# Expert results added onto two sums per token in HBM by accumulating transfers, in place of eight slot rows that are fetched and weighted at the end

## The reference, cut to what matters

```python
T, D, TOP_K, N_EXPERTS, EXPERT_HIDDEN, EXPERT_BLOCK = 512, 1024, 8, 64, 256, 128

def routed_experts(t, top_i, top_w, w_gu, w_dn):
    """Exact token-choice dispatch: sort assignments by expert, pad each expert segment to EXPERT_BLOCK rows."""
    ...
    def one_block(args):
        rb, e = args
        return swiglu_2(t_pad[rb], w_gu[e], w_dn[e]).astype(jnp.float32)

    ys = lax.map(one_block, (rows.reshape(n_blk, EXPERT_BLOCK), blk_expert)).reshape(P, D)
    out = jnp.zeros((T + 1, D), jnp.float32).at[rows].add(ys * wts[:, None])
    return out[:T]

# moe_ffn: routed + shared;  second_block:
x = x + g2 * moe_ffn(h, ...)
return rmsnorm_2(x, final_g)
```

## Time and profile before

| | |
|---|---|
| median of 3 runs | 3413.61 us (3406.23 to 3413.91) |
| the profiled execution | 3413.78 us |
| its span, first to last instruction | 3411.9 us |
| mean granted TensorE clock | 0.983 |
| TensorE busy | 3300.3 us (97%) |
| software queue (GpSimd's transfers) | 20736 packets, 33.60 MB |
| HBM written | 41.94 MB |

### The profile page before, as it was taken

The page is one execution under the profiler, slowest core; times in us unless marked ns, Lnnn a source line. Parts: engine busy times, 40 slices in busy tenths (PEclk is TensorE's granted clock), DMA queues, the critical chain, the costliest instruction groups (busy, mean ns, idle before and its releaser), DMA issues.

```text
span 3411.9 us, 48654 instructions
## 1 busy us (share of the span) xinstructions
PE 3300.3 (97%) x16474; PEld 2667.5 (78%) x16474; DVE 1978.3 (58%) x2520; ACT 1757.1 (52%) x2126; POOL 1335.7 (39%) x670
## 2 busy tenths in 40 slices
PE   8999999999999999999999999999999999999996
PEld 6888887778888788888678888787866788888784
DVE  4335674653354433541563333457766799999898
ACT  5552335455523555321645533414562688888884
POOL 3444441144444344444144444343202344444441
PEclk9999999999999999999999999899999999999998
DMA  3224331022253222533322233222102899999997
GB/s 124 98 95 167 113 102 50 20 92 94 97 169 121 86 98 93 165 119 117 125 80 97 93 97 100 74 93 90 32 7 73 320 381 382 389 387 389 374 366 295
DMA packets 128100, 534.42 MB, mean 157 GB/s; under 512 B 24464, under 2 KB 24720, under 8 KB 100112
## 3 DMA queue, kind: packets, MB, share of 16 engines
q1 hardware_dynamic: 107136, 499.63, 41.2%
q0 software_dynamic: 20736, 33.60, 2.6%
q10 hardware_dynamic: 144, 0.08, 0.0%
HBM read 531.64 MB, written 41.94 MB: 168 GB/s over the span
## 4 chain that ended last, share of the span: by engine, by line
PE 60%; issue 24%; POOL 7%; DVE 5%; ACT 1%; DMA 1%; POOLq 0%; DVEq 0%; SPq 0%; ACTq 0%
PE ps L822 16%; PE ps L824 16%; PE ps L823 16%; POOL w_lo L1893 7%; PE ps L1304 2%; PE ps L984 1%; PE ps L1109 1%; PE ps L842 1%; PE ps L1009 1%; PE ps L994 1%; PE ps L1127 1%; PE ps L1055 1%; PE ps L1088 1%; PE ps L1288 0%; DMA big<-in_exp_gu 0%
## 5 line engine op out<-in xcount | busy, mean ns | idle before, releaser
L1893 POOL TENSOR_TENSOR w_lo<-stage_buf,w_hi 128x1024 fp32r<-128x1024 f32 (+1 forms) x396 | 969.5, 2448 | 1511.6 <-ACT w_hi L1461 1511.6
L1461 ACT ACTIVATE w_hi<-stage_buf 128x1024 fp32r<-128x1024 f32 (+1 forms) x396 | 413.9, 1046 | 1189.6 <-PE ps L824 1133.6
L822 PE MATMUL ps<-x_hi,w_hi 128*128 128x512 f32 x1984 | 776.9, 392 | 6.8 <-POOL w_lo L1893 5.6
L823 PE MATMUL ps<-x_lo,w_hi 128*128 128x512 f32 x1984 | 775.4, 391 | 0.0
L824 PE MATMUL ps<-x_hi,w_lo 128*128 128x512 f32 x1984 | 775.0, 391 | 0.0
L822 PE MATMUL ps<-hid,w_hi 128*128 128x512 f32 x1312 | 518.8, 395 | 3.0 <-issue 1.7
L824 PE MATMUL ps<-hid,w_lo 128*128 128x512 f32 x1312 | 511.6, 390 | 0.0
L823 PE MATMUL ps<-hid,w_hi 128*128 128x512 f32 x1312 | 510.8, 389 | 0.0
L822 PEld LDWEIGHTS ps<-x_hi,w_hi 128*128 128x128 f32 x1984 | 374.6, 189 | 88.4 <-POOL w_lo L1893 6.7
L824 PEld LDWEIGHTS ps<-x_hi,w_lo 128*128 128x128 f32 x1984 | 374.6, 189 | 78.6
L823 PEld LDWEIGHTS ps<-x_lo,w_hi 128*128 128x128 f32 x1984 | 374.5, 189 | 77.4
(11 more groups left out here) (403 smaller groups left out, 4994.4 us busy)
## 6 DMA issues: line engine op xcount, KB each, us to landing
stage_buf<-in_gu SPq DMA_DIRECT2D x176, 512.0 KB, 3.2
big<-in_exp_gu SPq DMA_DIRECT2D x72, 1024.0 KB
h_buf<-in_exp_gu SPq DMA_DIRECT2D x72, 1024.0 KB
s_buf<-in_exp_dn SPq DMA_DIRECT2D x72, 1024.0 KB
stage_buf<-in_down SPq DMA_DIRECT2D x64, 512.0 KB, 3.6
stage_buf<-in_down SPq DMA_DIRECT2D x32, 384.0 KB, 3.2
sil_buf<-in_ada SPq DMA_DIRECT2D x24, 512.0 KB, 4.2
tmp_buf<-in_ada SPq DMA_DIRECT2D x24, 512.0 KB, 4.2
```

The source lines that it names most:

```text
L822: nc.tensor.matmul(o, a_hi, b_hi, start=start, stop=False)
L823: nc.tensor.matmul(o, a_hi, b_lo, start=False, stop=False)
L1461: nc.scalar.activation(w_hi[s][:, 0:n], stage[s][:, 0:n], ACT.Copy).then_inc(upper_done, 1)
L1893: nc.gpsimd.tensor_tensor(w_lo[s][:, 0:n], stage[s][:, 0:n], w_hi[s][:, 0:n].bitcast(F32), ALU.subtract).then_inc(parted, 1)
```

## The change

Two tensors of 512 x 1024 in HBM, `token_sums0` and `token_sums1`, take the place of `slot_rows`. GpSimd writes zeros to them from `xg[1]`, and writes the weights from `slot_w` to a third tensor, `pair_weights`. For each block a new indirect gather fetches the weight of each row into a column `w_col[s]`; ScalarE multiplies by it while it copies the result out of PSUM; and GpSimd's transfer adds the rows onto the token's row of the sum of that s (`compute_op=ALU.add`), where the scatter wrote rows of their own. A block holds a token at most once. The table gets a third column for the token number of the add.

At the end SP loads the two sums, TensorE adds them in PSUM with the plain identity (16 matmuls of 512 columns where there were 24), and VectorE has two instructions a tile in place of four; g2 and x are applied to the shared expert's output ahead of that. The early row additions and the scaled identities go.

The diff, without the declarations of semaphores and the removed lines that the words above cover:

```diff
@@ block_kernel: buffers
-        rows = ([big[:, 12288 + r * D:12288 + (r + 1) * D] for r in range(4)] +
-                [h_buf[:, r * D:(r + 1) * D] for r in range(4)] + [big[:, r * D:(r + 1) * D] for r in range(4, 12)])
+        sums = [[b[:, t * D:(t + 1) * D] for t in range(TT)] for b in (big[:, 12288:16384], h_buf)]
...
+        OUT_AT, W_AT = 5, 3
+        table = mask[:, 1024:1024 + 3 * (BLOCKS + OUT_AT)].rearrange("p (b c) -> p b c", c=3)
+        tab_f, tab_o = table[:, 0:BLOCKS, 0], table[:, OUT_AT:OUT_AT + BLOCKS, 1]
+        tab_v = table[:, W_AT:W_AT + BLOCKS, 2]
+        w_col = [mask[:, 1406 + s:1407 + s] for s in range(2)]
@@ sync
-                    def fetch(row, t, k, done):
-                        sp.dma_start(row.bitcast(I32), dr["slots"][t, :, k, :]).then_inc(done, 16)
...
                     for s in range(2):
+                        for j in range(2):
+                            after(raw_parted[j], more * 2 + (3 + s))
+                    for s in range(2):
+                        after(o_out[s], more * 16 + 32)
                         for t in range(TT):
+                            sp.dma_start(sums[s][t], dr[f"sum{s}"][t * P:(t + 1) * P, :]).then_inc(sum_in[s][t], 16)
@@ tensor: sum_rows
+                for s in range(2):
+                    for t in range(TT):
+                        pe.wait_ge(sum_in[s][t], 16)
                         for c in range(2):
+                            last = nc.tensor.matmul(ps[:, 2 * t + c, :], eye[:, :], sums[s][t][:, c * T:(c + 1) * T],
+                                                    start=(s == 0), stop=(s == 1))
+                        if s == 1:
+                            last.then_inc(fin["mm"], 1)
@@ scalar: evacuate
-                        nc.scalar.activation(o_sb[s], ps_t[:, b * T:b * T + D], ACT.Copy).then_inc(bk["oev"], 1)
+                        act.wait_ge(w_in[s], i * 16 + 16)
+                        nc.scalar.activation(o_sb[s], ps_t[:, b * T:b * T + D], ACT.Copy, scale=w_col[s]).then_inc(bk["oev"], 1)
...
-                    act.wait_ge(bk["tx"], more_n * 2 + 4)
-                    for j, w in enumerate(eye_w):
-                        n = j // 3 * TOP_K + EARLY + j % 3
-                        last = nc.scalar.activation(w, eye[:, :], ACT.Copy, scale=slot_w[:, n:n + 1])
@@ gpsimd
                     for s in range(2):
                         link(nc.gpsimd.memset(xg[s], 0.0))
+                        link(nc.gpsimd.memset(w_col[s], 0.0))
+                    for s in range(2):
+                        for t in range(TT):
+                            nc.gpsimd.dma_start(dr[f"sum{s}"][t * P:(t + 1) * P, :], xg[1]).then_inc(sums_set, 16)
                     pool.wait_ge(tab["in"], 2)
+                    nc.gpsimd.dma_start(dr["weights"].rearrange("(t p k) n -> p t (k n)", p=P, k=TOP_K),
+                                        slot_w.rearrange("p (t k) -> p t k", k=TOP_K)).then_inc(sums_set, 16)
...
-                    def scatter(s, at):
+                    def add_out(s, at):
+                        pool.sem_inc(bk["asked"], 1)
                         nc.gpsimd.indirect_dma_start(
-                            out=dr["slots"].rearrange("t p k n -> (t p k) n"),
-                            out_offset=bass.IndirectOffsetOnAxis(ap=idx[:, at, 1:2], axis=0),
-                            in_=o_sb[s].bitcast(I32), in_offset=None,
-                            bounds_check=T * TOP_K - 1, oob_is_err=False).then_inc(o_out[s], 16)
+                            out=dr[f"sum{s}"], out_offset=bass.IndirectOffsetOnAxis(ap=idx[:, at, 1:2], axis=0),
+                            in_=o_sb[s], in_offset=None,
+                            bounds_check=T - 1, oob_is_err=False, compute_op=ALU.add).then_inc(o_out[s], 16)
+
+                    def weight(s, at):
+                        nc.gpsimd.indirect_dma_start(
+                            out=w_col[s], out_offset=None, in_=dr["weights"],
+                            in_offset=bass.IndirectOffsetOnAxis(ap=idx[:, at, 2:3], axis=0),
+                            bounds_check=T * TOP_K - 1, oob_is_err=False).then_inc(w_in[s], 16)
...
+                        if s == 1:
+                            pool.wait_ge(sums_set, 16 * (2 * TT + 1))
                         gather(s)
...
-                    def one_block(i, s, first=False):
+                    def one_block(i, s, round_no):
                         pool.wait_ge(bk["tx"], i * 2 + (s + 2))
                         pool.sem_inc(bk["asked"], 1)
-                        if not first:
+                        if round_no >= 1:
                             evacuated(i * 2 + (s - 1))
-                        entry(1 - s, bass.ds(i * 2 + (s + 3), 1), i * 2 + (s + 4), 0, 1 if first else 2)
+                        entry(1 - s, bass.ds(i * 2 + (s + 3), 1), i * 2 + (s + 4), 0, 3)
                         gather(1 - s)
-                        if not first:
-                            scatter(s, 1 - s)
+                        weight(s, 1 - s)
+                        if round_no >= 1:
+                            add_out(s, 1 - s)
@@ vector: tables, combine
+                nc.vector.tensor_copy(tab_o, tab_f).then_inc(tab["in"], 1)
...
+                def gated_early(t):
+                    y = sh_tok[:, t, :]
+                    link(nc.vector.tensor_tensor(y, y, g2_row, ALU.mult))
+                    link(nc.vector.tensor_tensor(y, y, x_tok[:, t, :], ALU.add))
...
                     dve.wait_ge(fin["mm"], t + 1)
-                    dve.wait_ge(fin["row"], (EARLY - 1) * TT + t + 1)
-                    link(nc.vector.tensor_tensor(y, y, ps_t[:, 2 * t * T:2 * t * T + D], ALU.add))
-                    dve.wait_ge(row_last[t], 16)
-                    w = slot_w[:, t * TOP_K + 7:t * TOP_K + 8]
-                    link(nc.vector.scalar_tensor_tensor(out=y, in0=late_row[t, 7], scalar=w, in1=y, op0=ALU.mult, op1=ALU.add))
-                    link(nc.vector.tensor_tensor(y, y, g2_row, ALU.mult))
+                    link(nc.vector.tensor_tensor(x_tok[:, t, :], ps_t[:, 2 * t * T:2 * t * T + D], g2_row, ALU.mult))
                     nc.vector.tensor_tensor(y, y, x_tok[:, t, :], ALU.add).then_inc(fin["sum"], 1)
```

More of the change, by code:

```diff
@@ L445, in block_kernel @@
         o_out = [sem(f"o_out{s}") for s in range(2)]
[L446 to L449, removed]
+        sum_in = [[sem(f"sum_in{s}{t}") for t in range(TT)] for s in range(2)]
+        w_in = [sem(f"w_in{s}") for s in range(2)]
+        sums_set = sem("sums_set")
+        fin = {n: sem(f"fin_{n}") for n in ("mm", "sum", "std", "y")}
         RAW = 2048
@@ L734, in _ @@
                     for s in range(2):
[L735 to L740, removed]
-                        for t in range(TT):
-                            if k < 2 and t % 2 == 0:
-                                after(raw_parted[t // 2], more * 2 + (3 + k))
-                            fetch(rows[k * TT + t], t, k, row_in[k])
-                    for i, (t, k) in enumerate(LATE):
-                        if i == 0:
-                            for s in range(2):
-                                after(o_out[s], more * 16 + 16)
-                            after(o_out[0], more * 16 + 32)
-                        if k == 7 and t == 0:
-                            after(o_out[1], more * 16 + 32)
-                        sp.wait_ge(fin["row"], max(i, k == 4 and 4 * t) + 1)
-                        fetch(rows[i], t, k, row_last[t] if k == 7 else row_in[t])
+                        for j in range(2):
+                            after(raw_parted[j], more * 2 + (3 + s))
+                    for s in range(2):
+                        after(o_out[s], more * 16 + 32)
+                        for t in range(TT):
+                            sp.dma_start(sums[s][t], dr[f"sum{s}"][t * P:(t + 1) * P, :]).then_inc(sum_in[s][t], 16)
             if stop_at is None:
@@ L2728, in routed @@
                 hidden_low(1, more_n + 1)
-            def add_row(n):
-                k, t = n // TT, n % TT
-                if t == 0:
-                    dve.wait_ge(row_in[k], 64)
-                if k >= 1:
-                    dve.wait_ge(fin["row"], n - TT + 1)
-                w = slot_w[:, t * TOP_K + k:t * TOP_K + k + 1]
-                nc.vector.scalar_tensor_tensor(out=sh_tok[:, t, :], in0=rows[n], scalar=w, in1=sh_tok[:, t, :],
-                                               op0=ALU.mult, op1=ALU.add).then_inc(fin["row"], 1)
-            def combine():
-                for n in range(EARLY * TT):
-                    add_row(n)
+            def combine():
+                dve.wait_ge(moe["sh"], KD)
+                def gated_early(t):
+                    y = sh_tok[:, t, :]
+                    link(nc.vector.tensor_tensor(y, y, g2_row, ALU.mult))
+                    link(nc.vector.tensor_tensor(y, y, x_tok[:, t, :], ALU.add))
                 def add_late(t):
@@ L2762, in final_norm @@
                     ins.then_inc(fin["y"], 1)
```

(6 more changed lines are left out.)

31 lines of the change are left out of this document (9 added, 22 removed).

## The result

The changed kernel takes 3462.3 us, median of 4 runs (3461.39 to 3463.87). The kernel before, on the same chip, took 3409.9 us (4 runs, 3405.28 to 3413.91). The ratio is 1.016, 95% interval 1.015 to 1.017: slower by 52 us. The forecast was 3436, slower, with a range from 3399 to 3500; its sum has a loss of 22 us.

A forecast was written before the change was run, and what follows sets the result against it. The prediction took TensorE to set the routed blocks' pace, with the transfers nearly level. It summed 3413.8 us + 35 (routed blocks) + 1 (start) - 14 (tail) = 3436 us, slower, range 3399 to 3500.

The forecast's parts named there:

- So the transfers have a small reserve, some 8% on the mean: Routed blocks: DMA at 381 GB/s could reach the tail's 413, so TensorE sets the pace, nearly together with the transfers.
- I count it inside the 0.5: Routed blocks: the heavy stretch's bandwidth loss, up to 1 us a block, is covered by the 0.5 us a block.
- +35: Routed blocks: evacuations wait for an earlier transfer, 0.5 us in 70 of 72 blocks, bounds +17 to +56 us.
- The landing: Routed blocks: the add, issued 3.3 us later, lands 8.89 us plus 0.56 after its issue, so evacuations wait for it.
- The brake: Routed blocks: late evacuations let the weight gather in ahead of VectorE, shortening the chain by 3.3 us until waits rebuild.
- Rival 2: Routed blocks: the accumulate is much slower than a scatter, +60 us (3461) or +216 us (3617); chance 0.22.
- Rival 1: Routed blocks keep their pace as the add lands within 8.4 us; the tail's gain stays, 3401 us; chance 0.26.
- Start, +1: Start of the stage: zero writes fit GpSimd's idle time, the second gather waits for the weight table: +1 us (0 to +4).
- Tail, -14: After the last evacuation: fewer TensorE sums and half the VectorE instructions a tile save 14 us (10 to 16).
- Under 0.1 us: Routed blocks: ScalarE's scale operand and VectorE's one extra 100-column copy cost under 0.1 us.

The follow-up runs named there:

- e2: The changed kernel without the weight gather (constant weight 0.3125), the add kept: 3462.2 us, ratio 1.0152 to the kernel before.
- e5: e3 with one more plain load of 256 KB a block on SP's queue, onto 128 partitions: 3436.9 us, ratio 1.0079 to the kernel before.
- e3: The changed kernel without the add (plain scatter) and without the weight gather (constant weight): 3395.8 us, ratio 0.9956 to the kernel before.
- e10: The changed kernel with a block's rows spread over all 128 partitions, otherwise unedited: 3421.8 us, ratio 1.0047 to the kernel before.
- e6: e3 with a second gather of the block's token rows where the weight gather stood: 3463.1 us, ratio 1.0166 to the kernel before.
- e8: The changed kernel with constant weights and each add made twice, the second onto two further tensors: 3595.5 us, ratio 1.0543 to the kernel before.
- e1: The changed kernel without the addition (rows overwrite, plain scatter), weight gathers kept: 3399.7 us, ratio 0.9972 to the kernel before.
- e12: e10 without the weight gather (constant weight), the add kept: 3402.0 us, ratio 0.9984 to the kernel before.
- e14: e3 with the rows spread over the partitions, so neither add nor weight gather: 3399.0 us, ratio 0.9965 to the kernel before.
- e13: e10 with GpSimd's issues in the order weight gather, add, token gather: 3422.9 us, ratio 1.0056 to the kernel before.

## Why the prediction had the direction and not the cause

- **TensorE bounds, transfers near it: the reserve was misread.** The failed step is "So the transfers have a small reserve, some 8% on the mean", 381 against the 413 GB/s of the tail. The tail's fetches and the weights are plain transfers that use all partitions. Rows aren't: 0.47 MB of a block's 3.6 MB went at 246 GB/s (an estimate, from e2 and e5). The sum with that price is 9.44 us, all of the block, and one of the sixteen steps of each load was already late. e5 tests it: 0.262 MB more of plain load, which a reserve of 8% would have hidden (381 + 28 = 409 GB/s, below 413), cost 0.57 us a block. A mean over the rings, in bytes or in busy share, can't show such a reserve; about the same busy share went with 418 and 348 GB/s in the earlier trace rows.
- **"I count it inside the 0.5".** The added read was priced at 0.56 us by its bytes at 418 GB/s, and put into the chain of the landing, where the buffers two blocks deep take most of it. It belonged beside the weights, on the rings, at its full 0.89 us a block (e2 less e3), 63 us over 71 blocks. That is the +62.8 us where the sum has +35. "Slower" came out all the same, and partly by luck: the wait that carried the 35 us was hardly there.
- **The landing.** Every instant on GpSimd came out within 0.5 us, and the wait that was to follow did not: 1.8 us in all. The add's issue ends 0.4 us later than forecast because an accumulating issue takes 1.6 us by itself where the scatter took 1.0, a term that the prediction lacks. (In the earlier trace rows the scatter ends 0.86 us after the first VectorE instruction, not 0.94, which changes little.) The add lands 8.8 us after its issue ends (median of the 33 whose sixteen steps the trace has whole; forecast 9.45). Blocks at 10.32 us leave the chain through one buffer 20.6 us, more than the 20.02 that the forecast gave it. Once the rings were relieved, in e10, the block shortened and late evacuations came back, 25.7 us of waits; the one looked at above ended with the add's landing. In e6 and e8 it is the first wait of all. So the mechanism exists, in the kernel after behind a longer one.
- **The brake** had nothing to act on.
- **Rival 2** had the right size, 10.33 us a block and 3461, and half the reason: two reads per row on a full ring. Its price was worked out from a longer landing; what the runs show is late weight pieces, by the load on one part of the rings. That the two numbers agree is luck.
- **Rival 1** named a landing of 8.4 us as its point. e1, where the chain is the same but the add plain, shows that no wait arises there: its transfer lands 10.4 us after the start of its issue (median), 7.5 after the end, inside the 8.4. The time is 3399.7, rival 1's is 3401.
- **Start, +1:** +1.8, of the size of the scatter between executions, so that it neither confirms nor refutes the +1. The eight zero writes take 4.56 us of issues, not 8 to 10; the second gather waits for the weight table's write, 2.8 us.
- **Tail, -14:** -14.4, in the timeline of the kernel after:

```profile
3424.46 1.11 ACT L1827 ACTIVATE stage_buf<-ps,mask 128x1024 f32<-128x1024 f32 x1 [3.57 <-PE ps L806]
3427.23 1.72 POOL L1947 DMA_INDIRECT token_sums<-stage_buf,mask  x1 [0.92 <-POOL mask L1929]
3435.42 1.74 SPq L735 DMA_DIRECT2D h_buf<-token_sums  x4
3440.60 7.03 PE L1353 MATMUL ps<-h_buf,eye 128*128 128x512 f32 x16
3442.60 1.23 DVE L2737 TENSOR_TENSOR mixed_buf<-ps,rot 128x1024 f32<-128x1024 f32 x1 [11.30 <-PE ps L1353]
3458.24 0.74 DVE L2745 SCALAR_TENSOR_TENSOR mixed_buf<-xn_buf,small,rstd 128x512 f32<-128x512 f32 x1
```

The last add lands 8.2 us after its issue began, VectorE starts 18.1 us after the evacuation (forecast 18.1) and ends at 34.5 (forecast 34.7). The order is as forecast: add, load, sums, VectorE.
- **"Under 0.1 us"** for the scale and the third column: the evacuation takes 1.11 in place of 1.03, and e3's block is 0.06 us longer than before. Over 71 blocks that is some 4 us, a term that the sum doesn't have; no run takes it apart.

## What to carry to other kernels

A rate from another stretch is no ceiling for this one: price each kind of transfer by what it moves per us in the stretch itself, and test the reserve by one plain load more. A busy share that is a mean over all rings can hide one that is full; the last steps of a load's landing show it. Take a price only from two runs that wait for the same thing. An accumulating transfer costs its target's read too, which the profile's bytes don't show. When rows fill only some partitions, spread them before anything else is concluded about the transfers, and look next at the queue that issues them.

## What the runs showed of the hardware

- An accumulating indirect transfer takes of the rings' time what two plain row transfers take: its read 0.65 us of all rings' time, a further gather of the same rows 0.70 (e2, e6, e3).
- With 57 rows on neighbouring partitions a pass over 0.233 MB costs 0.95 us of a block, 246 GB/s (an estimate, from e2 and e5), at a busy share of 0.98; with the rows spread, the add's read costs 0.05 us of the block (e12 less e14). Presumably it fits into a reserve there; how large that is was not measured. A 256 KB load onto 64 partitions costs 2.2 us, at a granted clock of 0.96, onto 128 partitions 0.63 (estimated like the pass; 0.57 over e3).
- With packed rows the last of the sixteen steps of a weight load comes 6.5 us after the fifteenth (after), with spread rows 0.6 (e10). Which unit is overloaded stays open.
- GpSimd's issues take, when VectorE isn't reading two SBUF tiles as they start, 0.98 to 1.06 us for scatter, gather and weight gather and 1.6 us for an add (kernels before and after). Of those that start under such an instruction, most last longer: 2.6 us for the scatter and the weight gather, 2.3 for the gather (e13), 3.4 for the add (medians). An indirect issue also reads its row numbers from SBUF; the runs don't separate this read from the writing of the transfer's description.
